# A decoder block with latent and windowed attention: inputs laid out by load, shorter rotary tables, a shift moved to ACT, and a split last group

## The reference, cut to what matters

```python
mod = silu(c) @ ada_w + ada_b                 # sh1, sc1, ga1, sh2, sc2, ga2
h = rmsnorm(x, g1) * (1 + sc1) + sh1
q_lat, kv_lat, k_rope, q_s, k_s, v_s, gl_a, gl_b = split(h @ w_in)
y_mla = mla_attention(...)   # 8 heads: 64 plain + 32 rotary dims, causal over 4096 tokens
y_swa = swa_attention(...)   # 16 heads, window 128, sinks, relative bias
merged = sigmoid(gl_a + b) * (y_mla @ w_o_mla) + sigmoid(gl_b + b) * (y_swa @ w_o_swa)
x = x + ga1 * (merged @ w_o)
h = rmsnorm(x, g2) * (1 + sc2) + sh2          # "the second shift" is sh2
x = x + ga2 * (square(relu(h @ w_ff1)) @ w_ff2)
out = rmsnorm(x, g_final)
```

## Time and profile before

| | |
|---|---|
| median of 3 runs | 1395.92 us (1393.61 to 1542.28) |
| the profiled execution | 1395.63 us, span 1394.0 us |
| spans of the 8 cores | 1389.4 to 1394.0 us |
| granted TensorE clock, mean | 0.985 to 0.988 |
| first score product | 149.0 us |
| last product | ends at 1380.9 us, but for the sums of the final norm |

### The profile page before, as it was taken

How to read it: one execution, slowest core, us unless ns; L and a number is a source line. 1 busy time by engine, 2 the same in 40 slices (tenths; PEclk the granted TensorE clock), 3 DMA queues, 4 the chain that set the end, 5 groups by cost and what they waited for, 6 DMA issues and landing times.

```text
span 1394.0 us, 20354 instructions; the slowest of 8 cores (1389.4 to 1394.0 us)
## 1 busy us (share of the span) xinstructions
PE 1283.1 (92%) x7010; PEld 587.4 (42%) x7010; DVE 632.3 (45%) x860; ACT 655.7 (47%) x901; POOL 201.4 (14%) x174
## 2 busy tenths in 40 slices
PE   0778889999999899999999999999999999999996
PEld 0533444444444353232444444444444444444442
DVE  2578665666662114324222222664443443443356
ACT  0387778979889716849322222443003103202333
POOL 3000435220035101000233322010000000000000
PEclk9999899999999999999999999999999999999999
DMA  9982754130353205020442524386214204000014
GB/s 168 215 110 41 152 119 102 46 62 1 61 73 86 40 1 54 1 27 1 130 44 27 54 31 61 122 115 98 31 14 78 31 1 79 13 1 1 1 61 181
DMA packets 95250, 88.20 MB, mean 63 GB/s; under 512 B 36768, under 2 KB 79824, under 8 KB 95056
## 3 DMA queue, kind: packets, MB, share of 16 engines
q0 software_dynamic: 72640, 51.03, 27.3%
q1 hardware_dynamic: 22512, 35.89, 8.0%
HBM read 127.15 MB, written 8.41 MB: 97 GB/s over the span
## 4 chain that ended last, share of the span: by engine, by line
PE 81%; ACT 7%; issue 4%; DVE 3%; DMA 3%; SPq 1%; ACTq 0%; DVEq 0%; POOL 0%; another core or an unknown queue 0%; POOLq 0%
PE psb L452 81%; ACT arena L457 7%; DMA arena<-eoh 1%; SPq L275 1%; DVE arena L461 1%; DMA scr<-arena 1%; DVE arena L477 1%; DVE arena L473 1%; DMA arena<-xo 1%; DVE arena L469 0%; DVE arena L466 0%; ACTq L314 0%; DVEq L314 0%; ACT L457 0%; POOL arena L461 0%
## 5 line engine op out<-in xcount | busy, mean ns | idle before, releaser
L452 PE MATMUL psb<-arena 128*128 128x512 bf16 (+7 forms) x7010 | 1283.1, 343 | 99.9 <-ACT arena L457 34.4
L452 PEld LDWEIGHTS psb<-arena 128*128 128x128 bf16 (+4 forms) x7010 | 587.4, 100 | 795.3 <-issue 265.6
L457 ACT ACTIVATE arena<-psb 128x1024 bf16<-128x1024 f32 (+5 forms) x479 | 370.6, 822 | 124.5 <-PE psb L452 121.5
L457 ACT ACTIVATE arena<-psb,arena 128x512 f32<-128x512 f32 x220 | 150.7, 687 | 461.5 <-PE psb L452 396.1
L461 DVE TENSOR_TENSOR arena<-psb,arena 128x512 f32<-128x512 f32 (+4 forms) x228 | 148.0, 661 | 321.9 <-ACT arena L457 217.2
L461 DVE TENSOR_TENSOR arena<-arena 128x512 bf16<-128x512 f32 (+2 forms) x176 | 128.9, 732 | 143.7 <-ACT arena L457 136.3
L457 ACT ACTIVATE arena<-arena 128x512 f32<-128x512 f32 (+3 forms) x196 | 137.9, 716 | 104.6 <-DVE arena L473 69.6
L473 DVE SCALAR_TENSOR_TENSOR arena<-psb,arena 128x512 f32<-128x512 f32 x160 | 120.2, 751 | 138.7 <-PE psb L452 137.9
L477 DVE CAST arena<-psb 64x512 bf16<-64x512 f32 (+1 forms) x126 | 86.8, 689 | 119.4 <-PE psb L452 117.9
L461 POOL TENSOR_TENSOR arena<-arena 128x512 bf16<-128x512 f32 (+1 forms) x56 | 97.5, 1741 | 200.5 <-DVE arena L461 185.9
L473 DVE SCALAR_TENSOR_TENSOR arena<-arena 128x512 bf16<-128x512 f32 (+5 forms) x106 | 80.8, 769 | 4.4 <-ACT arena L457 1.8
(11 more groups left out here) (14 smaller groups left out, 28.9 us busy)
## 6 DMA issues: line engine op xcount, KB each, us to landing
arena<-w_ff POOLq DMA_DIRECT2D x16, 1024.0 KB, 12.0
arena<-ada_w POOLq DMA_DIRECT2D x12, 1024.0 KB, 14.3
arena<-xo SPq DMA_DIRECT2D x16, 512.0 KB, 4.2
arena<-xo SPq DMA_DIRECT2D x4, 2048.0 KB, 9.3
out<-arena SPq DMA_DIRECT2D x16, 512.0 KB, 2.8
arena<-xo POOLq DMA_DIRECT2D x4, 1024.0 KB, 32.3
arena<-xs POOLq DMA_DIRECT2D x4, 1024.0 KB, 32.5
arena<-xs SPq DMA_DIRECT2D x8, 512.0 KB, 4.2
```

The costliest lines, as they stand in the source:

```text
L452: S.op("pe", lambda e: e.matmul(out, lhsT=lhsT, rhs=rhs, start=start, stop=stop), reads=R, writes=Wr, sig=sig, cost=cost_of("pe", out, lhsT))
L457: S.op("act", lambda e: e.activation(out=out, in_=in_, func=func, **kw), reads=R, writes=Wr, cost=cost_of("act", out))
```

## The change

It does eight things.

1. Every large input lies in HBM as it is loaded: a partition's share of a load is one run (16 KB for a weight piece or a group of x), where it was 8 runs of 2 KB, or 4 of 4 KB for `w_ff2`. A merge piece is one DMA and no longer four. The output is laid out by group too.
2. `ada0` pieces 2 and 3 and the first group of x are issued ahead of pieces 0 and 1.
3. The rotary chain runs once (10 operations behind the first copy), and both Sin tables are taken from it.
4. Cos and sin lie in adjacent rows. A query keeps both products in 64 rows, without the sum, and the rotated keys are there twice (three small DMAs per group, `kdup`), so that a score contracts over 128 rows. `qr_build` has 2 DVE operations where it had 4, `x_group` 2 for the keys where it had 3.
5. The second half of a group's squares is always on DVE, which before was so for the other tokens only.
6. `sh2` is added by ACT in `h2_apply`: a product on DVE, then Identity with scale and bias on ACT, through the two buffers `rl` that `ff1_tile` uses. The one-column products with `sh2b`, the copy and the bias of Relu are gone.
7. In the last quarter of the MLP the last 512 tokens are two groups of 256.
8. The planner's costs are others, halo loads come one head later, and halo steps are spread differently.

```diff
-        for i in range(4):
-            S.dma("pool", ada0[i], kc_src(adaw_d, 512 * i, 512 * i + 512), ("ada0", i), writes=[("ada0", i)])
+        def ada0_load(i):
+            S.dma("pool", V(o_ada0 + i * 8192, BF16, 8 * 512), adaw_d[i], ("ada0", i), writes=[("ada0", i)])
+        for i in (2, 3):
+            ada0_load(i)
...
-        for i in range(NXB):
+        x_load(0)
+        for i in (0, 1):
+            ada0_load(i)
+        for i in range(1, NXB):
             x_load(i)
...
-            tt("dve", rt1[HA, :], PS(pb)[HA, :], tabO[HA, cs], ALU.mult, [("ps", pb), ("tabO", 0)], ["rt1"])
-            tt("dve", rt2[HA, :], PS(pb)[HB, :], tabO[HB, cs], ALU.mult, [("ps", pb), ("tabO", 1)], ["rt2"])
-            for e in range(2):
+            for e, hs in ((0, HA), (1, HB)):
                 qt, qk = q_tile(j, e)
-                rs_ = slice(32 * e, 32 * e + 32)
-                tt("dve", qt[R2, cs], rt1[rs_, :], rt2[rs_, :], ALU.add, ["rt1", "rt2"], [qk + (g, 1)])
+                tt("dve", qt[HB, cs], PS(pb)[hs, :], tabO[hs, cs], ALU.mult, [("ps", pb), ("tabO", 0), ("tabO", 1)],
+                   [qk + (g, 1)])
...
-            if own:
-                act(sq[:, 4:8, :], xb[:, 4:8, :], AF.Square, [xk], [("sq1", i % 2, 1)])
-            else:
+            if True:
                 tt("dve", sq[:, 4:8, :], xb[:, 4:8, :], xb[:, 4:8, :], ALU.mult, [xk], [("sq1", i % 2, 1)])
...
-            stt(rt2[R0, :], K_["t12"][R2, :], bvk[R2, 3:4], tab[R0, cs], ALU.add, ALU.mult,
-                [("t12", s_), "bvk", (tk, 1)], ["rt2"])
-            tt("dve", Kb[0][0][R2, ks], rt1[R0, :], rt2[R0, :], ALU.add, ["rt1", "rt2"],
-               [("Kpe0", 0, G)])
+            tt("dve", Kb[0][0][R2, ks], rt1[0:32, :], rt1[32:64, :], ALU.add, ["rt1"], [("Kpe0", 0, G)])
+            for (e, p0) in ((0, 96), (1, 64), (1, 96)):
+                S.dma("sp", Kb[0][e][p0:p0 + 32, ks], Kb[0][0][R2, ks], ("kdup", G), reads=[("Kpe0", 0, G)],
+                      writes=[("Kdup0", G)], group=True)
...
-                mm(out, Kb[b][e][0:96, 128 * t:128 * t + 128], qt[0:96, 512 * c + qo:512 * c + 512], True, mk is None,
+                mm(out, Kb[b][e][:, 128 * t:128 * t + 128], qt[:, 512 * c + qo:512 * c + 512], True, mk is None,
...
-                stt(h2[:, kc, cs], x1[:, kc, cs], gm2[:, kc:kc + 1], rst[g % 2], ALU.mult, ALU.mult,
-                    [("x1", g, kc), ("rst", g % 2), "mod2"], [("h2", g)])
+                rb = rctr[0] % 2
+                rctr[0] += 1
+                tt("dve", rl_[rb], x1[:, kc, cs], rst[g % 2], ALU.mult, [("x1", g, kc), ("rst", g % 2)], [("rl", rb)])
+                act(h2[:, kc, cs], rl_[rb], AF.Identity, [("rl", rb), "mod2"], [("h2", g)],
+                    scale=gm2[:, kc:kc + 1], bias=sh2[:, kc:kc + 1])
...
-                for fl in range(4):
-                    for kc in range(8):
-                        mm(PS(7)[:, fg0 + fl:fg0 + fl + 1], w[:, kc, 128 * fl:128 * fl + 128], sh2b[:, kc:kc + 1],
-                           kc == 0, kc == 7, [slot_key(s), "sh2b"], [("ps", 7)])
...
+                if last:
+                    segs[3:] = [(1536, 256), (1792, 256)]
```

More of the change, by code:

```diff
@@ L115, in arrange @@
         for i in range(n - 1, -1, -1):
-            own = tasks[i]["cost"] + tasks[i]["bytes"] / 180e3
+            own = tasks[i]["cost"] + tasks[i]["bytes"] / (190e3 if tasks[i]["e"] == "pool" else 370e3)
             tail[i] = own + max([tail[j] + LAT for j in succ[i]], default=0.0)
@@ L464, in ts @@
         def ts(eng, out, in0, s1, s2, op0, op1, R, Wr):
-            if s2 is None:
+            if eng == "dve":
+                n = 1
+                for x in out.shape[1:]:
+                    n *= x
+                S.op(eng, lambda e: e.tensor_scalar(out=out, in0=in0, scalar1=s1, scalar2=s2, op0=op0, op1=op1) if s2
+                     is not None else e.tensor_scalar(out=out, in0=in0, scalar1=s1, scalar2=None, op0=op0),
+                     reads=R, writes=Wr, cost=0.1 + 0.00061 * n)
+            elif s2 is None:
                 S.op(eng, lambda e: e.tensor_scalar(out=out, in0=in0, scalar1=s1, scalar2=None, op0=op0),
@@ L634, in build_program @@
         mm(PS(6)[0:16, 0:128], relT[0:32, :], eoh[0:32, :], True, True, ["relT", "eoh"], [("ps", 6)])
-        for i in range(4):
+        for i in (2, 3, 0, 1):
             ada_mm(i, ada0[i], ("ada0", i))
@@ L659, in build_program @@
         o_kvn = A.alloc(S_LEN * 2, 1, 3, "kvn")
-        o_K = [A.alloc(2 * S_LEN * 2, 1 + 2 * b, 3 + 0.5 * b, "K%d Kpe%d" % (b, b)) for b in range(2)]
+        o_K = [A.alloc(2 * S_LEN * 2, 1 + 2 * b, 3 + 0.5 * b, "K%d Kpe%d Kdup%d" % (b, b, b)) for b in range(2)]
         kvn = V(o_kvn, BF16, S_LEN)
@@ L934, in build_program @@
         ho_load(1)
-        for (b, e) in ((0, 1), (1, 0), (1, 1)):
-            S.dma("sp", Kb[b][e][R2, :], Kb[0][0][R2, :], ("kpe", b, e), reads=[("Kpe0", 0, G) for G in range(8)],
-                  writes=[("Kpe%d" % b, e, G) for G in range(8)] if (b, e) != (0, 0) else [])
+        for e in range(2):
+            S.dma("sp", Kb[1][e][HB, :], Kb[0][0][HB, :], ("kpe", e),
+                  reads=[("Kpe0", 0, G) for G in range(8)] + [("Kdup0", G) for G in range(8)],
+                  writes=[("Kpe1", e, G) for G in range(8)])
         def ada_piece(i):
@@ L1081, in build_program @@
                         do_step()
-                if first and c == 0 and h == 6:
+                if first and c == 0 and h == 7:
                     late_loads()
@@ L1424, in build_program @@
                 last = hf == 3
-                order = [(m, g) for g in range(4) for m in range(8)] if last else \
-                    [(m, g) for m in range(8) for g in range(4)]
-                for (m, g) in order:
-                    cs = slice(512 * g, 512 * g + 512)
+                if last:
+                    segs[3:] = [(1536, 256), (1792, 256)]
+                order = [(m, q) for q in range(len(segs)) for m in range(8)] if last else \
+                    [(m, q) for m in range(8) for q in range(4)]
+                for (m, q) in order:
+                    c0, w = segs[q]
+                    g, cs = c0 // 512, slice(c0, c0 + w)
                     pb = 2 + it2 % 5 if last else 4 + it2 % 3
@@ L1566 @@
         b, half = core // 2, core % 2
-        oT = np.asarray(res.results[core]["out"], np.float32)
+        oT = np.asarray(res.results[core]["out"], np.float32).transpose(2, 1, 0, 3).reshape(D, T)
         for lc, gc in enumerate(OWN_BLOCKS[half]):
```

237 lines of the change are left out of this document (120 added, 117 removed).

## The result

The changed kernel takes **1426.5 us**, median of 6 runs (1416.7 to 1478.6), against 1396.4 for the kernel before (6 runs). Some executions on eight cores run one die at a lower clock; with those left out on both sides the ratio is 1.018, 95% interval 1.012 to 1.025. Three of the changed kernel's runs lie together at 1416.7 to 1416.8 us; the fourth that counts, 1436.3, is the profiled one. So the change costs some 20 to 25 us where 40 us less were forecast. In the profiled execution the granted clock of cores 4 and 5 was 0.96 and that of the others 0.98 to 0.99, so I read **core 2** in both traces: 1389.5 us before, 1413.8 after.

The account below looks back on a forecast made before the run. PE, busy for 92% of the span, bounds the kernel; the start is bound by loads to about 78 us, then three busy engines. Start 25, MLP 12, latent stage 2, end 1: 40 us less, 1356 us against 1395.6, range 1335 to 1378.

Parts of the forecast that it names:

- The speed: The start's loads: all 12 pieces move 5% faster with longer runs, 10% allowed.
- The start: the loads: x's first group, now third on its queue, gains 16 us; sh1 comes near 50 us, biases complete near 57.
- With a queue that is never empty: Start: last group of x lands at 104 us, 99 with the gain; 35.5 us cut by a fifth follow, giving 127.
- It is the DMA engines that are full (share 1.14): Between 29.9 and 75 us DMA engines are full, not PE, DVE or ACT; loads bind the start to about 78.
- 124 us: End of the start: first score product at 124 us, before 149.0; 25 us less, bounds 110 to 138 us.
- rival (a): The start is bound by engines, not loads; it ends at 138 us, total time 1370 us; chance 0.17.
- 256 x 45 ns: MLP: 256 dropped one-column products at 45 ns each save 12 us, bounds 8 to 16.
- I take nothing: MLP: the new DVE product and ACT Identity hide behind PE; 0 to 3 us in the first tiles, counted as nothing.
- The latent stage and the end: Latent stage 2 us less (10 less to 6 more); end 1 us less (5 less to 2 more).
- (d): Identity is not in ACT's loaded table, so table loads in each tile make the kernel slower, 1426 us; chance 0.04.
- Slower: Whole kernel: slower than before by more than the 2% band; chance 0.04.
- The signs: Named as proof against the prediction: first score after 135 us, or PE waiting on ACT between 865 and 930 us.

Follow-up runs that it names:

- e7: The kernel before, with only the start's twelve loads (ada0 pieces, x groups) in runs of 16 KB: 1428.1 us, ratio 1.021.
- e9: The changed kernel, with the start's ada0 pieces and x groups read from arrays that lie as in the kernel before: 1398.0 us, ratio 1.000.
- e14: The changed kernel, with adabT, gains, hv, relT, eoh and sinks issued on POOL's queue ahead of the casts, not on SP's: 1403.0 us, ratio 1.003.
- e16: e15 with the start's pieces read as in the kernel before, in runs of 2 KB: 1386.5 us, ratio 0.992.
- e15: e14 with the old order of the ada0 pieces and DVE's last h2_apply product one tile ahead in the MLP: 1375.9 us, ratio 0.985.
- e13: Changed kernel, start's old arrays, old ada0 order, early products behind bvk, DVE a tile ahead, second half of x's loads left out: 1376.1 us, ratio 0.984.
- e3: The changed kernel, with ada_w and x stored so that pieces are read in runs of 2 KB: 1401.5 us, ratio 1.003.
- e6: e3 with ada0 pieces 0 to 3 loaded and multiplied in their old order, ahead of x: 1401.0 us, ratio 1.003.
- e12: The kernel before without the MLP's 256 one-column products, their copies and Relu's bias, nothing in their place: 1392.2 us, ratio 0.996.
- e4: The changed kernel, with DVE's last h2_apply product one tile earlier in the MLP, in two buffers of its own: 1409.7 us, ratio 1.009.
- e5: The changed kernel, with the last h2_apply products in two buffers of their own, instruction order unchanged: 1420.2 us, ratio 1.016.

## Why the prediction was wrong

- **"The speed" (5% on the casts).** Right in sign and too low: the eighth piece landed at 64.5, 15% sooner than core 2's 75.8. But the term left out its other side. I priced the layout only on the queue that got it. "The start: the loads" had the biases complete near 57 us, which takes the loads of SP's queue at their old times; they came as much as 30 us later, the float32 products began at 82.5 (39.7 before), and the biases were complete at 96. This is the step that failed: 25 us less became 24 more. e7 (30 us on the kernel before) and e9 (19 us back on the changed one) show the cause, e14 to e16 that it is long runs beside another queue's small loads, and not long runs as such.
- **"With a queue that is never empty" (last group at 99 us), then 35.5 us "cut by a fifth".** Both parts failed, and they are the other half of the step. The queue was empty for long: its first eight loads had landed by 64.5, and the last was issued at 123.4, when its slot came free, and landed at 134.1. In the rows it was the same, issued at 102.0. And the stretch behind it did not shrink: 34.4 us before, 36.0 after, 35.2 in e15 (104.3 to 139.5), 35.1 in e16, 36.0 in e9. The freed time of DVE and ACT did not show in it.
- **"It is the DMA engines that are full (share 1.14)".** True, and it was the warning: on full engines a faster queue takes its time from another. I read it only as "loads bound the start", without asking which of the two queues PE, DVE and ACT were waiting for. PE's first wait before was for eoh on SP's queue.
- **"124 us."** Wrong also where nothing starves: 148.1 in e9, 142.3 in e13, 139.5 in e15. Packing at 0.82 of the fullest engine from 57 us on was too hopeful; rival (a), 138 us, is about what the best version reached. The order of pieces (x third) gave nothing at 2 KB (e3 against e6), and beside long runs it seems to have cost 14 to 20 us (e14 against e15, not run alone): `sh1` then stands on DVE behind the tables' copies, for which DVE waits 15.1 us in e14.
- **"256 x 45 ns."** Mechanism right, size off: 6.0 us for 11.5 (e12). The period minus 512 products at their ideal rate counted as one-column work what belongs to the full products: the changed kernel's period, with none of the small ones, is 110.5 and not 109.2 us, 215.8 ns a product. The low bound of 8 was too high as well. The Trainium skill's rule for a weight load (page TensorE: Matmul & The Clock Gate, section LDWEIGHTS (loading the stationary operand)), weighed there at 107 ns each, is further off still; e12 has 23 ns.
- **`h2_apply`: "I take nothing", of 0 to 3 us.** It cost 7 us (e4; 8.7 in the trace). I added up busy times, 1.3 and 1.4 against 1.7 us, where the two engines run in turns: DVE product, Identity, Relu, DVE square, each in order behind the other. Their sum is what a tile takes. The reason I named, shared buffers, is not it (e5).
- **The latent stage and the end.** 1.3 us less for 2, about 2 less for 1; within the bounds. That DVE ends some 2.5 us behind PE was not seen: from PE's last product to the end it is 3.4 us shorter, and the price is paid by PE, 2.5 us of short waits for ACT where it had 1.3.
- **Rivals.** (d) named a time that happens to be close, but not for its reason: six table loads before, six after. None of the rivals had the transfer side. "Slower" got 0.04; it deserved far more, as the change touched the one resource that was full.
- **The signs.** The first score after 135 us was named as a sign of being wrong, and it came (170.1). The other one, PE waiting for ACT between 865 and 930 us, did not: those waits lie at 961 to 973. No table load was added. In the last two groups PE waited for ACT, not for DVE.

The parts now add up: layout +19 (e9), tiles of the MLP +7 (e4), dropped products -6 (e12), end -2, latent stage -1, and 2 to 3 us in the start of e9, gives 19 to 20 over before, where 1416.8 lies 20.5 over the 1396.3 measured beside it.

Open: why e3 and e9 differ by 3.5 us and why the first piece lands 5 to 7 us later in both than before, though its runs are as long. The old order of the ada0 pieces was not tried alone at 16 KB, nor the planner's new costs alone.

## What to carry to other kernels

When one queue's transfers get longer runs, look at what shares the DMA engines with it: a queue of small packets gets one packet for each long one, and its loads, priced at nothing before, become the critical path. Put the small loads that open the program ahead of the bulk, on the bulk's own queue, and let nothing urgent stand in an engine's order behind what is still on the slow queue; then the long runs pay. Before you count on a queue that is never empty, see in the rows what releases its last loads. And where two in-order engines hand a tile back and forth, add their times and do not compare each with PE's; writing one producer a tile ahead removes the turn-taking.

## What the runs showed of the hardware

- On full DMA engines the two queues moved packets one for one (227 and 231 in 10 us, 7.3 and 0.5 KB each), and 221 and 220 in e7. A 16 KB load, behind others of its own queue, took 44.7 us to land beside runs of 16 KB and 16.8 beside 2 KB; ahead of the runs of 16 KB on their queue it took 7.0.
- A one-column product costs 23 to 25 ns between full ones; a full product of 512 columns 215.8 ns. 32 one-column products in a row took 0.99 us, 31 ns each.
- PE was idle for 6.16 us up to 972.64. Its granted clock was 0.88 from 965 to 970 us, 0.50 from 970 to 975 and 0.93 from 975 to 980.
- With runs of 2 KB taken from 2 MB without gaps the kernel took 3.5 us more than with the same runs 8 and 24 KB apart (e3, e9; e3 has other edits too).
